# A decoder step on one core: the relative-position bias moves from matmuls to a VectorE addition, and attention's value products are issued for two pairs of heads at a time

## Chip, core and metric

The kernel runs on one core of a Trainium2 chip. The metric is the device time of one execution in microseconds (us). The engines are TensorE (PE; its weight loads are shown as PEld), VectorE (DVE), ScalarE (ACT), GpSimd (POOL) and SyncE (SP), which issues most transfers.

## The reference, cut to what matters

One hybrid layer: an input projection, sparse attention beside a gated linear recurrence (HGRN2), and an output projection. For the 1024 prompt rows, attention adds a relative-position bias to the logits of the keys that are kept:

```python
logits = jnp.einsum('btngd,btknd->btngk', qg, k_sel).astype(F32) * HEAD_DIM ** -0.5
bias = rel_table.astype(F32)[t5_bucket(q_pos[None, :, None] - idx)]   # 32 buckets, the last one from distance 128 on
logits = jnp.where(valid[:, :, None, None, :], logits + bias, -jnp.inf)
p = jax.nn.softmax(logits, axis=-1)
out = jnp.einsum('btngk,btknd->btngd', p.astype(v_sel.dtype), v_sel)
...
mix = jnp.concatenate([a_out * silu(a_gate), h_n * silu(h_gate)], axis=-1)
return x + jnp.einsum('bte,ed->btd', mix, w_out)
```

There are 8 query heads on 4 key/value heads. A bias that is the same for all far keys drops out of the softmax, so only the two 128-key blocks nearest to a query tile need one. Eight decode rows (the sample) go through the same layer against a paged cache.

## The kernel before

Everything up to about 560 us is projections, index search and recurrence. The change lives in what follows, `pe_tail`, `act_tail`, `dve_tail`, `gp_tail` and `sp_tail`, one instruction stream written out by hand for each engine and tied by semaphores.

The prompt's attention is a loop over **steps** m = 0 to 63. A step is one head (h = m mod 8) of one tile of 128 queries, t = 7 - m // 8, with the causal width of 128 (t + 1) keys, so the first eight steps are the widest (1024 keys) and the last eight the narrowest (128). In step m each engine does, in its own order:

- TensorE: the **scores** of head m + 1 (`scores`, L1139: keys as high and low part, `KA` L1154 and `KB` L1160, and between them two matmuls that add the bias, L1158, from `BH` and `BL`, its high and low part, against the antidiagonal matrix `ANR`); in odd steps from 3 on the **value products** of one pair of heads (`values`, L1178, matmuls on L1191); in some odd steps sample work (page keys L1251 in steps 3 to 15, page values L1294 in steps 25 to 35); the **transposes** of head m's probabilities (L1175); then the other sample work (`SIDE`), mixing (`mix`, L1195) and, from step 41, output products (`out`, L1210, matmuls on L1222). The last 23 groups of output products follow the loop.
- VectorE: the **maximum** of head m (L1093: adds the mask, writes the logits back to PSUM and reduces), for odd m from 19 on the copy of the transposed probabilities of head m - 1's turn (L1107), then its sample work: in the first dozen steps one round of a search of bits (`sample_keep` L928, `sample_try` L920), each of which waits for a small matmul on TensorE (L1235) that stands behind the transposes of the step.
- ScalarE: the **exponentials** of head m (L862), behind them the **copy** of the transposed probabilities of head m - 1 from PSUM (L874; in the steps where VectorE doesn't do it).

The scores of head m + 1 wait for the exponentials of head m - 1 (two halves of PSUM take turns). The transposes of head m wait for its exponentials and for the copy of head m - 1 (L1168 to L1170). A copy waits until its buffer, one of three (`PTS`), has been read by the value products. These read two heads:

```python
if m >= 3 and m % 2 == 1:
    values((m - 3) // 2)
```

The bias table leaves a matmul of L2042 as 8 rows of 383 distances, is stored to DRAM by SP (`bias_spill`, L1356, early in the program) and comes back spread over 128 partitions (L601). ScalarE rounds it (`act_bias`, L814) and VectorE takes the rest (L966) while the queries and keys are built (`dve_builds`), ahead of step 0.

## Time and profile before

| | us |
|---|---|
| median of 3 runs | 857.04 (856.95 to 860.72) |
| profiled execution, its own time | 857.15 |
| its span (first to last instruction) | 854.8 |
| TensorE busy in the span | 819.4 (96%) |
| VectorE busy | 570.8 (67%) |
| ScalarE busy | 410.6 (48%) |
| granted TensorE clock, mean | 1.0 of full speed |

A busy share is an average over stages with different limits. Matmuls are pipelined: the duration shown of one is its latency, and what it costs the engine is the distance from its start to the next one's.

### The profile page before, as it was taken

To read this page: it belongs to the slowest core of one execution; us is meant where nothing else is said; L and a number is where in the kernel's file an instruction comes from. 1 tells how busy PE (TensorE), PEld (TensorE's weight loads), DVE (VectorE), ACT (ScalarE), POOL (GpSimd) and SP (SyncE) were. 2 spreads that over 40 slices of the span, in tenths; PEclk is the share of its full clock that TensorE was granted. 3 is DMA by queue.
4 is the path that set the end of the run, shared out by engine and by line. 5 is a ranking of instruction groups with operands and counts; after the bars stand their busy time and mean duration, and the time that the engine had idled before them with its cause. 6 is when DMAs were issued, how large, how long until landed. Compare 5 with 4: busy or idle time off the path is not lost.

```text
span 854.8 us, 17930 instructions
## 1 busy us (share of the span) xinstructions
PE 819.4 (96%) x6497; PEld 741.2 (87%) x6497; DVE 570.8 (67%) x1153; ACT 410.6 (48%) x1200; POOL 384.0 (45%) x575
## 2 busy tenths in 40 slices
PE   3999989999999999999999999989999998999998
PEld 3989979699999989999999999956677667898998
DVE  4535777899988988859993536787856358555111
ACT  6646674224554496467455645554445345422100
POOL 2543635209824484549565425139731327501400
PEclk9999999999999999999999999999999999999999
DMA  8312102201101312041205145494653535341422
GB/s 268 80 38 60 62 27 68 76 21 50 51 2 50 98 53 75 26 130 39 82 26 150 37 117 150 130 257 124 158 161 122 162 99 167 107 142 45 142 76 75
DMA packets 69179, 81.31 MB, mean 95 GB/s; under 512 B 20234, under 2 KB 55738, under 8 KB 68842
## 3 DMA queue, kind: packets, MB, share of 16 engines
q1 hardware_dynamic: 64410, 66.58, 25.5%
q0 software_dynamic: 4688, 13.64, 5.8%
q8 instruction: 52, 0.85, 0.4%
q14 instruction: 29, 0.24, 0.1%
HBM read 62.85 MB, written 17.34 MB: 94 GB/s over the span
## 4 chain that ended last, share of the span: by engine, by line
PE 79%; issue 5%; DVE 4%; POOL 4%; ACT 3%; SPq 3%; DMA 2%; POOLq 0%; ACTq 0%; DVEq 0%
PE psum L2095 25%; PE psum L2092 15%; PE psum L1222 12%; PE psum L1991 4%; PE psum L2029 3%; PE psum L1175 3%; PE psum L1191 2%; PE psum L1294 2%; SPq L547 2%; PE psum L1975 2%; PE psum L2011 1%; PE psum L1158 1%; PE psum L1154 1%; PE psum L1160 1%; POOL page_keys L566 1%
## 5 line engine op out<-in xcount | busy, mean ns | idle before, releaser
L2095 PE MATMUL psum<-w_high,xT_high 128*128 128x256 f32 x720 | 204.1, 283 | 1.4 <-ACT psum L1672 1.4
L2095 PE MATMUL psum<-w_low,xT_high 128*128 128x256 f32 x720 | 201.9, 280 | 0.0
L2095 PE MATMUL psum<-w_high,xT_low 128*128 128x256 f32 x720 | 201.6, 280 | 0.0
L1878 DVE TENSOR_SCALAR_CACHE_REDUCE flag<-scores,candidate 128x384 f16<-128x384 f32 (+2 forms) x192 | 181.6, 946 | 6.8
L512 POOL TENSOR_TENSOR w_low<-w_raw,w_high 128x256 fp32r<-128x256 f32 (+1 forms) x168 | 123.0, 768 | 78.5 <-ACT w_high L1560 69.3
L2095 PEld LDWEIGHTS psum<-w_high,xT_high 128*128 128x128 f32 x720 | 127.4, 177 | 3.9 <-ACT psum L1672 1.6
L2095 PEld LDWEIGHTS psum<-w_low,xT_high 128*128 128x128 f32 x720 | 127.6, 177 | 2.3
L2095 PEld LDWEIGHTS psum<-w_high,xT_low 128*128 128x128 f32 x720 | 127.4, 177 | 2.4
L2092 PE MATMUL psum<-xT_high,w_high 128*128 128x384 f32 (+3 forms) x312 | 102.1, 327 | 1.6 <-DVE xT_low L1805 1.2
L2092 PE MATMUL psum<-xT_high,w_low 128*128 128x384 f32 (+3 forms) x312 | 99.7, 319 | 0.0
L2092 PE MATMUL psum<-xT_low,w_high 128*128 128x384 f32 (+3 forms) x312 | 99.6, 319 | 0.0
L862 ACT ACTIVATE prob<-psum,neg_max 128x1024 f32<-128x1024 f32 (+7 forms) x64 | 47.4, 740 | 98.9 <-DVE neg_max L1093 98.5
L1222 PE MATMUL psum<-w_high,xT_high 128*128 128x256 f32 (+1 forms) x288 | 81.9, 284 | 0.0
L1222 PE MATMUL psum<-w_low,xT_high 128*128 128x256 f32 (+1 forms) x288 | 80.7, 280 | 0.0
L1222 PE MATMUL psum<-w_high,xT_low 128*128 128x256 f32 (+1 forms) x288 | 80.6, 280 | 0.0
L1667 ACT ACTIVATE stage<-psum 128x256 f32<-128x256 f32 (+1 forms) x72 | 27.6, 385 | 86.4 <-PE psum L2095 76.8
L2092 PEld LDWEIGHTS psum<-xT_high,w_high 128*128 128x128 f32 (+1 forms) x312 | 57.6, 185 | 2.9 <-issue 1.2
L1462 POOL DMA_INDIRECT index_keys_T<-in_cache_ikt,index_page_rows x32 | 34.6, 1083 | 56.6 <-DMA index_keys_T<-in_cache_ikt,index_page_rows 55.7
L2092 PEld LDWEIGHTS psum<-xT_low,w_high 128*128 128x128 f32 (+1 forms) x312 | 57.6, 185 | 0.9
L2092 PEld LDWEIGHTS psum<-xT_high,w_low 128*128 128x128 f32 (+1 forms) x312 | 57.5, 184 | 0.5
L1093 DVE CUSTOM_DVE_ANT_0 psum<-psum,mask 128x1024 f32<-128x1024 f32 (+5 forms) x48 | 43.0, 898 | 19.1 <-PE psum L1160 18.4
L1003 DVE TENSOR_TENSOR y_rows<-psum,x_res 128x256 f32<-128x256 f32 (+1 forms) x36 | 15.1, 420 | 56.7 <-PE psum L1222 56.7
(313 smaller groups left out, 1853.5 us busy)
## 6 DMA issues: line engine op xcount, KB each, us to landing
w_raw<-in_w_main SPq DMA_DIRECT2D x40, 512.0 KB, 3.8
x_rows<-in_x_prompt SPq DMA_DIRECT2D x8, 512.0 KB, 5.6
page_keys<-in_cache_kt SPq DMA_DIRECT2D x32, 128.0 KB, 3.5
page_keys<-in_cache_kt POOLq DMA_DIRECT2D x32, 128.0 KB, 5.1
page_values<-in_cache_v SPq DMA_DIRECT2D x32, 128.0 KB, 3.7
page_values<-in_cache_v POOLq DMA_DIRECT2D x32, 128.0 KB, 3.4
x_res<-in_x_prompt SPq DMA_DIRECT2D x32, 128.0 KB
out<-y_rows SPq DMA_DIRECT2D x32, 128.0 KB
```

The lines of the kernel that those rows point to most:

```text
L512: last = gp.tensor_tensor(WL[:, u % 2, 4 * h + k, 0:w], WR[:, h, k, 0:w], f(WH[:, u % 2, 4 * h + k, 0:w]), ALU.subtract)
L862: act.activation(PB[:, m % 3, 0:w], ps(2 * (m % 2), w), ACT.Exp, scale=-1.0, bias=NB[:, h:h + 1], accum_out=RS[:, t % 2, h:h + 1]).then_in ...
L1093: dve.tensor_tensor_reduce(lg, lg, mask, -HD ** -0.5, 3e38, ALU.add, ALU.min, accum_out=NB[:, h:h + 1])\
L1175: last = pe.transpose(ps(4, P, o=b * P), PB[:, m % 3, b * P:(b + 1) * P], IDN[:, :])
L1222: last = pe.matmul(ps(OBANK[y], UW, rows(i)), a[:, k, row0(i):row0(i) + rows(i)], ww[:, sl, k, :], start=k == 0 and a is XH and ww is WH, ...
L1462: gp.indirect_dma_start(dst, None, cache_ikt.rearrange("a d k -> (a d) k"), bass.IndirectOffsetOnAxis(ap=PGX[:, col:col + 1], axis=0))\
L1667: last = act.activation(STG[0:r, g % 4, :], ps(bank, UW, r), ACT.Silu if kind in ("gh", "ga") else ACT.Copy)
L1878: dve.tensor_scalar(JK[:, 0:w], sc, threshold(k), None, op, ALU.add, accum_out=CNT[:, k:k + 1]).then_inc(s["dve_chain"], 1)
L1991: pe.matmul(ps(bank, 2 * SUB, w, o=2 * SUB * i), KT[:, o + c * w:o + (c + 1) * w], QT[:, :, c * P + i * SUB:c * P + (i + 1) * SUB], start= ...
L2029: last = pe.matmul(ps(4 + 2 * (m % 2) + c0 // 512, w), IQS[:, h, (t - 2) * P:(t - 1) * P], stack[:, c0:c0 + w], start=kk == 0, stop=kk == 1)
L2092: last = pe.matmul(ps(BANK[n], cw, m_), ww[:, sl, k, i * P:i * P + m_], x[:, k, t0:t0 + cw], start=first, stop=final)
L2095: last = pe.matmul(ps(BANK[n], w, rows(i)), x[:, k, row0(i):row0(i) + rows(i)], ww[:, sl, k, 0:w], start=first, stop=final)
```

## The change

TensorE no longer adds the bias. The table is stored to DRAM 128 times, once for each row of a tile, so that it can be read back with each row shifted by one (`BT`, in float32, in place of `BRAW`), and VectorE adds it to the scores in PSUM ahead of each maximum, waiting for that addition to end (`link`). ScalarE's rounding, VectorE's remainder, `ANR` and its load go away. In the space that is free, two more buffers of transposed probabilities stand (five), and the value products of two pairs of heads are issued together in the steps 5, 9, ... 61, the last two pairs behind the loop.

```diff
-        VT, BH, PT0, PT1, _e = over(H0, ("values_T", [NT, UW], F32), ("bias_high", [AH, NEAR], F32R),
-                                    ("pT_0", [NT, P], F32), ("pT_1", [NT, P], F32))
+        VT, PT3, PT4, PT0, PT1, _e = over(H0, ("values_T", [NT, UW], F32), ("pT_3", [NT, P], F32), ("pT_4", [NT, P], F32),
+                                          ("pT_0", [NT, P], F32), ("pT_1", [NT, P], F32))
-        PTS = [PT0, PT1, PT2]
+        PTS = [PT0, PT1, PT2, PT3, PT4]
-        d_ut = nc.dram_tensor("bias_spill", [AH, UL], F32)
+        d_ut = nc.dram_tensor("bias_spill", [AH, P, UL], F32)
...
-                sp.dma_start(BRAW[:, :, :], bass.AP(d_ut, 0, [[1, P], [UL, AH], [1, NEAR]])).then_inc(s["bias_in"], 16)
+                sp.dma_start(BT[:, :, :], bass.AP(d_ut, P - 1, [[UL - 1, P], [P * UL, AH], [1, NEAR]])).then_inc(s["bias_in"], 16)
...
-        def act_bias(act):
-            act.wait_ge(s["bias_in"], 16)
-            act.wait_ge(s["intra_products_ready"], NT * NG)
-            act.activation(BH[:, :, :], BRAW[:, :, :], ACT.Copy).then_inc(s["bias_high_ready"], 1)
...
-                    ge(act, s["attn_values_done"], (m1 - 1) // 2)
+                    ge(act, s["attn_values_done"], (m1 - 3) // 2)
...
-                if i == NT - 3:
-                    dve.wait_ge(s["bias_high_ready"], 1)
-                    dve.tensor_tensor(BL[:, :, :], BRAW[:, :, :], f(BH[:, :, :]), ALU.subtract).then_inc(s["bias_low_ready"], 1)
...
                     lg = ps(2 * (m % 2), P * (t + 1))
+                    k0, w = max(t - 1, 0) * P, min(t + 1, 2) * P
+                    if m == 0:
+                        dve.wait_ge(s["bias_in"], 16)
+                    link(dve.tensor_tensor(lg[:, k0:k0 + w], lg[:, k0:k0 + w], BT[:, h, NEAR - w:NEAR], ALU.add))
...
                     pe.matmul(ps(bank, n, o=c0), q, KA[:, h // 2, c0:c0 + n], start=True, stop=False)
-                    k0, k1 = max(c0, (t - 1) * P), min(c0 + n, (t + 1) * P)
-                    if k0 < k1:
-                        for half in (BH, BL):
-                            pe.matmul(ps(bank, k1 - k0, o=k0), ANR[:, :],
-                                      half[:, h, k0 - (t - 1) * P:k1 - (t - 1) * P], start=False, stop=False)
...
-                if m >= 3 and m % 2 == 1:
+                if m >= 5 and m % 4 == 1:
+                    values((m - 5) // 2)
                     values((m - 3) // 2)
...
+            values(NA // 2 - 2)
             values(NA // 2 - 1)
...
-            sp.dma_start(d_ut.ap(), UT[0:AH, :]).then_inc(s["bias_table_out"], 16)
+            sp.dma_start(d_ut.ap(), rep(UT[0:AH, :], P)).then_inc(s["bias_table_out"], 16)
```

TensorE, step 5 before: the scores of head 6 with their bias matmuls, then the first value products of heads 2 and 3 (pair 1; `pT_166` and `pT_185` are buffers of transposed probabilities).

```order
L1154 MATMUL psum<-kT_high,qT_stack 128x512
L1160 MATMUL psum<-kT_low,qT_stack 128x512
L1154 MATMUL psum<-kT_high,qT_stack 128x512
L1158 MATMUL psum<-bias_high,antidiagonal_r 128x256
L1158 MATMUL psum<-bias_low,antidiagonal_r 128x256
L1160 MATMUL psum<-kT_low,qT_stack 128x512
L1191 MATMUL psum<-pT_166,values_T 64x128
L1191 MATMUL psum<-pT_185,values_T 64x128
```

The same place of the changed kernel, whose own line numbers the rows show (L1146 and L1147 are the scores, L1178 the value products): the scores of head 6, then the first value products of heads 0 and 1 (`pT_183` and `pT_184` are buffers again).

```order
L1146 MATMUL psum<-kT_high,qT_stack 128x512
L1147 MATMUL psum<-kT_low,qT_stack 128x512
L1146 MATMUL psum<-kT_high,qT_stack 128x512
L1147 MATMUL psum<-kT_low,qT_stack 128x512
L1178 MATMUL psum<-pT_183,values_T 64x128
L1178 MATMUL psum<-pT_184,values_T 64x128
```

The bias matmuls are gone, and the pair that comes here is pair 0, which stood in step 3.

TensorE, step 5 before, where the value products end and the page keys begin.

```order
L1191 MATMUL psum<-pT_185,values_T 64x128
L1191 MATMUL psum<-pT_166,values_T 64x128
L1191 MATMUL psum<-pT_185,values_T 64x128
L1251 MATMUL psum<-page_keys_156,q_padded 32x512
L1251 MATMUL psum<-page_keys_157,q_padded 32x512
```

In the changed kernel, where the value products of heads 0 and 1 end, those of heads 2 and 3 follow.

```order
L1178 MATMUL psum<-pT_184,values_T 64x128
L1178 MATMUL psum<-pT_164,values_T 64x128
L1178 MATMUL psum<-pT_181,values_T 64x128
L1178 MATMUL psum<-pT_164,values_T 64x128
L1178 MATMUL psum<-pT_181,values_T 64x128
```

So step 5 holds 32 value products before and 64 now; the steps 3 and 7 hold none.

VectorE before, at the heads 0 to 2: the last product of the sample's new key, then the maximum of heads 0 and 1 (ISA, `neg_max`), and the first round of the search.

```order
L1011 TENSOR_TENSOR square<-q_rows_sample,k_rows_sample 8x4x64 x2
L1014 TENSOR_REDUCE new_key_scores<-square 8x8
L1093 ISA psum,neg_max<-psum,mask 128x1024
L1093 ISA neg_max 128x1
L1093 ISA psum,neg_max<-psum,mask 128x1024
L1093 ISA neg_max 128x1
L922 TENSOR_SCALAR candidate<-bits_so_far,candidate_bits,sign_flip 64x1
L924 TENSOR_SCALAR flag_sample,count<-scores_sample,candidate 64x1025
```

VectorE of the changed kernel at the same place (L1084 is the new addition, L1086 the maximum).

```order
L1000 TENSOR_TENSOR square<-q_rows_sample,k_rows_sample 8x4x64 x2
L1003 TENSOR_REDUCE new_key_scores<-square 8x8
L1084 TENSOR_TENSOR psum<-psum,bias_by_row 128x256
L1086 ISA psum,neg_max<-psum,mask 128x1024
L1086 ISA neg_max 128x1
L1084 TENSOR_TENSOR psum<-psum,bias_by_row 128x256
L1086 ISA psum,neg_max<-psum,mask 128x1024
L1086 ISA neg_max 128x1
L914 TENSOR_SCALAR candidate<-bits_so_far,candidate_bits,sign_flip 64x1
L916 TENSOR_SCALAR flag_sample,count<-scores_sample,candidate 64x1025
L918 TENSOR_SCALAR enough<-count 64x1
```

Ahead of each maximum now stands one addition over the two near blocks, 256 wide (128 in the last eight steps).

## Rows read from the trace of the kernel before

**Rows 1.** The page's first line: the span of the profiled execution.

```profile
span 854.8 us, 17930 instructions
```

**Rows 2.** Busy time by stretch: the loop (to 786 us) in three parts.

```profile
560.50:702.00 141.50, 133.62 (x1180) 96.71 (x1181) 89.98 (x189) 63.27 (x115) 66.16 (x121) 1.00 0.53 152
702.00:714.60 12.60, 9.64 (x89) 8.29 (x89) 10.64 (x19) 7.57 (x15) 6.71 (x7) 1.00 0.46 148
714.60:786.00 71.40, 68.89 (x611) 63.56 (x610) 40.85 (x108) 23.39 (x74) 24.31 (x24) 1.00 0.36 114
```

**Rows 3.** Timeline of TensorE in steps 3 to 5: start, us, [idle before].

```profile
577.45 0.33 PE L1175 MATMUL psum<-ident,prob 128*128 128x128 f32 x1
...
578.59 0.50 PE L1154 MATMUL psum<-kT_high,qT_stack 128*128 128x512 f32 x1
...
579.39 0.28 PE L1158 MATMUL psum<-bias_high,antidiagonal_r 128*128 128x256 f32 x1
579.51 0.28 PE L1158 MATMUL psum<-bias_low,antidiagonal_r 128*128 128x256 f32 x1
...
579.86 0.27 PE L1175 MATMUL psum<-ident,prob 128*128 128x128 f32 x1
...
582.46 0.33 PE L1191 MATMUL psum<-pT,values_T 128*64 128x128 f32 x2
...
584.36 0.62 PE L1251 MATMUL psum<-page_keys,q_padded 128*32 128x512 f32 x2
...
586.20 0.33 PE L1175 MATMUL psum<-ident,prob 128*128 128x128 f32 x1
```

**Rows 4.** Bias matmuls by source line: count, median ns, forms; one half of two.

```profile
L1158 PE MATMUL psum<-bias_high,antidiagonal_r x72: 220/279/288, 561.5 to 774.3; 128*128 128x256 f32 x48, 128*128 128x128 f32 x24
```

**Rows 5.** Timeline of TensorE, two bias matmuls 128 wide.

```profile
765.00 0.27 PE L1158 MATMUL psum<-bias_high,antidiagonal_r 128*128 128x128 f32 x1
765.11 0.27 PE L1158 MATMUL psum<-bias_low,antidiagonal_r 128*128 128x128 f32 x1
```

**Rows 6.** Timeline of VectorE: a search round begins, and the next maximum.

```profile
578.70 0.16 DVE L931 TENSOR_SCALAR bit_kept<-psum 64x1 int32<-64x1 f32 x1 [2.41 <-PE psum L1235]
...
580.97 1.23 DVE L1093 CUSTOM_DVE_ANT_0 psum<-psum,mask 128x1024 f32<-128x1024 f32 x1
```

**Rows 7.** Timeline of ScalarE: exponentials of one head, copy of another.

```profile
582.34 1.11 ACT L862 ACTIVATE prob<-psum,neg_max 128x1024 f32<-128x1024 f32 x1 [2.73 <-DVE neg_max L1093]
...
583.45 1.01 ACT L874 ACTIVATE pT<-psum 128x1024 f32<-128x1024 f32 x1
```

**Rows 8.** The page's groups: VectorE's nearest addition (count, busy, mean ns, idle before).

```profile
L1003 DVE TENSOR_TENSOR y_rows<-psum,x_res 128x256 f32<-128x256 f32 (+1 forms) x36 | 15.1, 420 | 56.7 <-PE psum L1222 56.7
```

**Rows 9.** Timeline ahead of step 0: VectorE's remainder, TensorE's first scores.

```profile
549.76 2.29 DVE L966 TENSOR_TENSOR bias_low<-bias_raw,bias_high 128x2048 fp32r<-128x2048 f32 x1
...
560.77 0.47 PE L1154 MATMUL psum<-kT_high,qT_stack 128*128 128x512 f32 x1 [0.96 <-DVE qT_stack L948]
```

**Rows 10.** Timeline of SP's queue around the bias table's store.

```profile
64.76 0.32 SPq L1356 DMA_DIRECT2D bias_spill<-bias_by_distance  x1
91.43 4.38 SPq L471 DMA_DIRECT2D w_raw<-in_w_main  x2
```

**Rows 11.** Timeline, places where TensorE waits (four) and GpSimd (one).

```profile
611.89 0.62 PE L1251 MATMUL psum<-page_keys,q_padded 128*32 128x512 f32 x2 [1.83 <-DMA page_keys<-in_cache_kt]
...
650.86 0.30 PE L1175 MATMUL psum<-ident,prob 128*128 128x128 f32 x1 [1.08 <-ACT pT L874]
...
702.00 0.63 PE L1207 MATMUL psum<-ident,agate_in 128*128 128x128 f32 x4 [0.36 <-ACT out_by_head L842]
...
707.89 1.29 POOL L743 TENSOR_TENSOR hgate_in<-hgate_in,hgrn_gain 128x512 f32<-128x512 f32 x1 [18.54 <-DMA agate_in<-agate_spill]
...
713.78 0.30 PE L1207 MATMUL psum<-ident,agate_in 128*128 128x128 f32 x1 [1.77 <-issue]
```

**Rows 12.** The chain that ended last: its last piece.

```profile
786.65 65.25 PE psum L1222 x552
```

More of the change, by code:

```diff
@@ L35 @@
 NEAR = 2 * P
-CONSTS_IN = 14 * 16
+CONSTS_IN = 13 * 16
 UL = 383
@@ L131 @@
 NUMBERS_AT = UNITS.index(("hg", 1))
-BIAS_AT = JOB0[LAST] + 12
 QUERIES_AT = JOB0[LAST] + 15
@@ L205, in hymba_step @@
         IDN = sb("ident", [P])
-        ANR = sb("antidiagonal_r", [P], F32R)
         QG = sb("q_gain", [HD])
@@ L329, in hymba_step @@
         assert _e <= cur[0]
-        TRF, ANT, _ = over(cur[0], ("causal_add_f", [P], F32), ("antidiagonal", [P], F32))
+        TRF, = over(cur[0], ("causal_add_f", [P], F32))[:1]
         VN, PN, DG, _e = over(cur[0] - 2048, ("v_new", [UW], F32), ("prob_new", [BR], F32), ("diag", [BR], F32))
@@ L350, in hymba_step @@
         RSM, _e = over(H0, ("relu_sample", [PAST + 1], F32))
-        BRAW, = over(R0_, ("bias_raw", [AH, NEAR], F32))[:1]
-        BL, = over(R0_, ("bias_low", [AH, NEAR], F32R))[:1]
-        VT, BH, PT0, PT1, _e = over(H0, ("values_T", [NT, UW], F32), ("bias_high", [AH, NEAR], F32R),
-                                    ("pT_0", [NT, P], F32), ("pT_1", [NT, P], F32))
+        BT, = over(R0_, ("bias_by_row", [AH, NEAR], F32))[:1]
+        VT, PT3, PT4, PT0, PT1, _e = over(H0, ("values_T", [NT, UW], F32), ("pT_3", [NT, P], F32), ("pT_4", [NT, P], F32),
+                                          ("pT_0", [NT, P], F32), ("pT_1", [NT, P], F32))
         assert _e <= cur[0], (_e, cur[0])
-        PTS = [PT0, PT1, PT2]
+        PTS = [PT0, PT1, PT2, PT3, PT4]
         PSA = ctx.enter_context(nc.psum_tensor("psum", [P, 8 * 512], F32))
@@ L873, in act_tail @@
                             act.wait_ge(s[f"rows_out{x}"], ALLS[x])
-                    act.activation(PTS[m1 % 3][:, :, :].rearrange("p b t -> p (b t)")[:, 0:w], ps(4, w), ACT.Copy)\
+                    act.activation(PTS[m1 % 5][:, :, :].rearrange("p b t -> p (b t)")[:, 0:w], ps(4, w), ACT.Copy)\
                         .then_inc(s["probs_T_act_ready"], 1)
@@ L1105, in dve_tail @@
                     dve.wait_ge(s["probs_transposed"], m1 + 1)
-                    ge(dve, s["attn_values_done"], (m1 - 1) // 2)
-                    dve.tensor_copy(PTS[m1 % 3][:, :, :].rearrange("p b t -> p (b t)")[:, 0:w], ps(4, w))\
+                    ge(dve, s["attn_values_done"], (m1 - 3) // 2)
+                    dve.tensor_copy(PTS[m1 % 5][:, :, :].rearrange("p b t -> p (b t)")[:, 0:w], ps(4, w))\
                         .then_inc(s["probs_T_dve_ready"], 1)
@@ L1144, in scores @@
                     pe.wait_ge(s["job_copied"], JOB0[NU])
-                    pe.wait_ge(s["bias_low_ready"], 1)
                     pe.wait_ge(s["masks_ready"], 6)
@@ L1191, in values @@
                         last = pe.matmul(ps(7, P, (g + 1) * HD, g * HD, kv * P), VT[:, b, kv * HD:(kv + 1) * HD],
-                                         PTS[(2 * p + g) % 3][:, b, :], start=b == 0, stop=b == t)
+                                         PTS[(2 * p + g) % 5][:, b, :], start=b == 0, stop=b == t)
                 last.then_inc(s["attn_values_done"], 1)
@@ L1310, in pe_tail @@
                     scores(m + 1)
-                if m >= 3 and m % 2 == 1:
+                if m >= 5 and m % 4 == 1:
+                    values((m - 5) // 2)
                     values((m - 3) // 2)
-                    for side in SIDE.get(m, ()):
-                        if side[0] in ("keys", "values"):
-                            sample(*side)
+                for side in SIDE.get(m, ()):
+                    if side[0] in ("keys", "values"):
+                        sample(*side)
                 transposes(m)
@@ L1346, in _ @@
                              (INM[:, :, :], c_masks[:, 0:256]),
-                             (HM[0:BR, :], c_masks[0:BR, 656:674]), (TRF[:, :], c_masks[:, 400:528]), (ANT[:, :], c_masks[:, 528:656])):
+                             (HM[0:BR, :], c_masks[0:BR, 656:674]), (TRF[:, :], c_masks[:, 400:528])):
                 sp.dma_start(dst, src).then_inc(s["const_in"], 16)
@@ L1477, in _ @@
             gp.wait_ge(s["const_in"], CONSTS_IN)
-            gp.tensor_scalar(ANR[:, :], ANT[:, :], 1.0, 0.0, ALU.mult, ALU.add)
             gp.tensor_scalar(E8B[0:8, :], E8[0:8, :], 1.0, 0.0, ALU.mult, ALU.add)
@@ L1752, in _ @@
                         chunk(*event)
-                    if n == BIAS_AT:
-                        act_bias(act)
                     if n in BUILD_AT:
```

## The prediction

> **What bounds the kernel now.** I read the chain that ended last first, then busy time by stretch, then TensorE's waits, and then the timelines of TensorE, VectorE and ScalarE side by side. The profiled span is 854.8 us [rows 1]. The reader is to see a loop that TensorE nearly fills but not quite: from 560.5 to 702.0 it is busy for 133.6 of 141.5 us, from 702.0 to 714.6 for 9.6 of 12.6, from there to 786.0 for 68.9 of 71.4 [rows 2]. So some 13 of 225 us are idle; all else that the change takes from TensorE is real time, if the other engines keep up. Behind the loop stands one block of output products of 65.25 us at the end of the chain [rows 12], which the change doesn't touch.
>
> One step of the widest tile shows how close the others are. The transposes of step 3 start at 577.45, the scores of head 5 at 578.59, the transposes of step 4 at 579.86; the value products of step 5 start at 582.46, its page keys at 584.36, its transposes at 586.20 [rows 3]. From step 3's transposes to step 5's it is 8.75 us, without a wait. In the same time VectorE does two search rounds of 2.27 us (578.70 to 580.97) and two maxima of 1.37 us (580.97 to ScalarE's start at 582.34) [rows 6, 7], 7.3 us in all. ScalarE needs 1.11 us for the exponentials and 1.01 for the copy behind them [rows 7].
>
> **What leaves TensorE.** 144 bias matmuls (two halves of 72): 96 are 256 wide, 48 are 128 wide [rows 4]. A wide one costs 0.12 us (579.39 to 579.51) [rows 3], a narrow one 0.11 (765.00 to 765.11) [rows 5]: 96 × 0.12 + 48 × 0.11 = **16.8 us**, 0.24 us in a usual step. That is the ceiling of the gain.
>
> **What comes to VectorE.** 64 additions in PSUM. The trace has no such operation; the nearest is an addition of a PSUM tile 256 wide to one in SBUF, 0.42 us [rows 8]. The range per addition: 0.35 (if its end overlaps what follows) to 0.5 (the wait for its end, of which I see up to 0.05 between tied VectorE instructions). I take 0.46, since it is the same read and the same width, tied to its successor: 64 × 0.46 = 29 us of VectorE time, less the remainder of 2.29 us [rows 9]. It stands in the path of every head: scores, addition, maximum, exponentials, transposes.
>
> **What moves.** The pairs 0, 2, 4, ... come two steps later, the others stay. Before, a pair's 1.9 us (582.46 to 584.36) lay between scores and transposes in every second step, and covered that path for both neighbours. Now it covers one step in four with 3.8 us, and the steps m = 3, 7, 11, ... have nothing unless sample work stands there. The five buffers never make a copy wait: it asks for the pair before the last but one.
>
> **What is nearly free.** The table's store grows from 12 KB to 1.57 MB at 64.76 us; SP's next transfer is at 91.43 [rows 10], so 26 us cover it. If the cover failed, the weights behind it would come as late as the store ends after that. The load keeps its size. Ahead of step 0, VectorE loses 2.29 us, but the last query tile needs TensorE's transposes first, and TensorE waited only 0.96 us there [rows 9]: I give 0.3. ScalarE's rounding and GpSimd's copy of the antidiagonal lie beside TensorE's projections: 0.
>
> **The sum, stretch by stretch** (a minus is earlier than before):
>
> Search steps, from step 5's transposes to step 9's. Before, two periods of 8.75 us: 17.4, the second a little shorter. After, from the end of step 5's transposes: round 5's result reaches VectorE at 0.15, a round 2.27, addition and maximum 1.8, exponentials 1.15 and copy 1.1 on ScalarE (the copy of head 6 stands behind the exponentials of head 7), transposes 0.95: step 7 ends at 7.4. Step 8 follows by the same queues: VectorE is still behind, its next round, addition and maximum end at 8.0, exponentials and copy at 10.1, transposes at 10.9. Step 9 has score 0.95, two pairs 3.8, page keys 1.84, transposes 0.85: 18.35. So these four steps become **0.95 slower**, though TensorE lost 0.95 us of work: the missing 1.9 is waits in steps 6 to 8. The first steps come out 1.2 late at step 5 and so +2.3 at step 9.
>
> Step 11 resets this. Before, TensorE waited 1.83 us for page keys until 611.89 [rows 11]; the pages depend on GpSimd's own work and not on the change. Now pair 4 (1.7 us) isn't in the way, so TensorE is there in time and leaves at the same 611.9, but owes pair 4: ±0.
>
> Steps 12 to 21. Scores save 10 × 0.24 = 2.4. The owed pair costs 1.7. Waits come at 12 (round, addition, maximum: 0.9), at 14 and 15 (0.4), at 19 and 20 (0.5 + 0.3) and at 21 (0.4): 2.5. Before, the transposes of step 21 start at 650.86 behind a wait of 1.08 [rows 11]. After: 2.5 + 1.7 - 2.4 = **+1.8**.
>
> Steps 22 to 35. Page values (1.83 us each) stand in every odd step from 25 on and cover the path. 14 steps save 14 × 0.24, and the tile with keys split at 512 saves 0.12 more in 8 of them: 4.3 us, of which two waits keep 0.9. Pair 17's neighbour (1.0) is deferred past step 35. So the last page values end 2.5 us early, **-2.5** where 702.00 stood [rows 11].
>
> Steps 36 to 39. TensorE's mixing at 713.78 waited 1.77 us; behind it stand GpSimd (18.54 us of waiting for `agate_in` until 707.89) and a VectorE operation [rows 11], a chain of transfers that starts when the last page values are copied out. It moves with that, so it stays at -2.5, and what the scores save here (1 us) is waited away.
>
> Steps 40 to 63. 24 × 0.23 = 5.3 us of scores leave. Against it: VectorE was without a pause behind the mixing and gets three additions there (+0.85); the steps 43 and 47 have no value products and only 0.7 to 1.6 us of TensorE work against a path of 2.0 + 0.46 (some 2 us); steps 45 and 49 wait 0.4 each; the one-block steps are covered by output products and keep 3 of their gain, but 1.5 of that ends in the step 51, 57 and 61 waits. Together about **+0.5**.
>
> Sum: -0.3 is absorbed at step 11; -2.5 + 0.5 = **-2 us**. Against the profiled execution's own 857.15, which is 0.1 above the median of 857.04, that gives 855. Its own range, from the two prices of the addition (0.35: some 2 us less in the uncovered steps; 0.5: 1 us more) and from the waits I followed (± 3 us): 850 to 859.
>
> **The rivals.**
>
> *The saving is mostly kept.* TensorE is busy for 94% of the first stretch and 96% of the last [rows 2], and VectorE has 51 of 141 us free there. If additions fit in its pauses and paths overlap better than I followed, 8 to 14 of the 16.8 us stay: 843 to 849, say 846. Against it: the cycle above. It decides if steps 6 to 8 show no wait of over 0.3 us.
>
> *VectorE and the path become the bound.* In the first stretch VectorE was busy 90.0 us; 36 additions of 0.46 make it 106.6 of 141.5. If every step without value products waits the addition's full 0.46 and, in addition, the 0.95 us that half a pair gave it, the 48 such steps lose 48 × 0.46 = 22, less 16.8: +5, 862; with two thirds of the steps waiting, the point from which it decides against the kernel, ±0 less 2. For it: the search steps. Against it: page values, page keys and output products cover half the steps. The Trainium skill (Perfetto Trace Analysis, Identifying the Most-Contended Engine) judges TensorE by the busy share of its weight loads rather than of its matmuls. The weight loads are busy 96.7 of 141.5 us [rows 2], 68%, against VectorE's 64% before and 75% after; by that page VectorE would then be the engine to relieve, and the time would come out as here, 862. No row before can show it.
>
> *It does nothing.* The waits at 611.89 and 713.78 [rows 11] are of transfers. If the page values' transfers, too, set the end at 702.00, step 36 starts where it did, and the loop behind it comes out even: 857.
>
> **How the numbers follow.** Forecast, -2: 0.50. Saving kept: 0.20. VectorE the bound: 0.20. Nothing: 0.10. A difference of over 0.5% (4.3 us) is about what a measurement of this kernel can tell from no change. Faster than that: the second case whole and 0.13 of the first, 0.33. Slower: 0.15 of the third case, and 0.01 of the first, 0.16. The rest is 0.51. The range 847 to 861 leaves out a good half of the second case and a third of the third, 0.2 in all.
>
> **What would show it.** Right: VectorE's additions at 0.40 to 0.48 us, 64 of them; TensorE's groups of L1154 and L1160 unchanged and 144 matmuls fewer; in the steps 7, 8 and 12 waits of TensorE for the copies of L874 of 1 us and more; page keys of step 11 at about 611.9 again; page values done about 2.5 us earlier; the block of 65.25 us unchanged. Wrong: TensorE's wait for L874 in total no larger than before (then the saving stays), or waits behind L1222 in the steps from 41 on of more than 3 us (then it is slower), or a late weight load near 91 us.

## The result: 3.7% slower, in two parts

The changed kernel takes 890.8 us (median of four executions, 885.25 to 895.11) against 857.3 for the kernel before. The ratio is 1.037, 95% interval [1.034, 1.040]. The forecast was 855 us, range 847 to 861: wrong in sign and in size. The profiled execution has a span of 893.2 us, against 854.8 [rows 1]. It is the slowest of the four (895.11 us), so the two parts below, read from it, add up to 38.4 us and not to the 33.5 of the medians.

**Part one lies ahead of the loop.** TensorE's first scores, which stood at 560.77 [rows 9], now start at 586.55, 25.8 us later, behind the same wait of 0.96 us for the same instruction of VectorE. Timeline of TensorE, changed kernel, the start of the loop (start, us, instruction, [idle before <- releaser]; a row with xN groups N instructions):

```profile
586.55 0.47 PE L1146 MATMUL psum<-kT_high,qT_stack 128*128 128x512 f32 x1 [0.96 <-DVE qT_stack L940]
...
587.10 0.39 PE L1146 MATMUL psum<-kT_high,qT_stack 128*128 128x512 f32 x1
587.33 0.40 PE L1147 MATMUL psum<-kT_low,qT_stack 128*128 128x512 f32 x1
...
591.04 1.43 PE L1162 MATMUL psum<-ident,prob 128*128 128x128 f32 x8 [2.40 <-ACT prob L854]
...
592.92 0.80 PE L1146 MATMUL psum<-kT_high,qT_stack 128*128 128x512 f32 x1
593.51 0.63 PE L1147 MATMUL psum<-kT_low,qT_stack 128*128 128x512 f32 x1
593.93 0.63 PE L1146 MATMUL psum<-kT_high,qT_stack 128*128 128x512 f32 x1
...
599.09 1.06 PE L1162 MATMUL psum<-ident,prob 128*128 128x128 f32 x8 [1.88 <-ACT pT L866]
...
603.68 1.91 PE L1238 MATMUL psum<-page_keys,q_padded 128*32 128x512 f32 x8 [2.29 <-DMA page_keys<-in_cache_kt]
```

Such a delay must be traced back to where it begins. GpSimd's timeline shows it: the gathers of index keys (each waits for the one before), between the weight work of two units.

```profile
64.89 1.00 POOL L1451 DMA_INDIRECT index_keys_T<-in_cache_ikt,index_page_rows  x1 [0.15 <-issue]
69.99 0.94 POOL L1451 DMA_INDIRECT index_keys_T<-in_cache_ikt,index_page_rows  x1 [4.10 <-DMA index_keys_T<-in_cache_ikt,index_page_rows]
86.41 1.18 POOL L1451 DMA_INDIRECT index_keys_T<-in_cache_ikt,index_page_rows  x1 [15.48 <-DMA index_keys_T<-in_cache_ikt,index_page_rows]
99.97 0.94 POOL L1451 DMA_INDIRECT index_keys_T<-in_cache_ikt,index_page_rows  x1 [12.39 <-DMA index_keys_T<-in_cache_ikt,index_page_rows]
102.68 1.84 POOL L1451 DMA_INDIRECT index_keys_T<-in_cache_ikt,index_page_rows  x1 [1.77 <-DMA index_keys_T<-in_cache_ikt,index_page_rows]
...
113.08 3.09 POOL L509 TENSOR_TENSOR w_low<-w_raw,w_high 128x256 fp32r<-128x256 f32 x3
```

The kernel before at the same place: the first and the last of the gathers behind 70 us, and the weight work behind them.

```profile
71.94 0.94 POOL L1462 DMA_INDIRECT index_keys_T<-in_cache_ikt,index_page_rows  x1 [1.88 <-DMA index_keys_T<-in_cache_ikt,index_page_rows]
...
85.77 1.12 POOL L1462 DMA_INDIRECT index_keys_T<-in_cache_ikt,index_page_rows  x1 [1.77 <-DMA index_keys_T<-in_cache_ikt,index_page_rows]
86.92 8.51 POOL L512 TENSOR_TENSOR w_low<-w_raw,w_high 128x256 fp32r<-128x256 f32 x8
```

And SP's queue of the changed kernel with the store, and the next weight load behind that work:

```profile
66.14 0.81 SPq L1345 DMA_DIRECT2D bias_spill<-bias_by_distance  x1
117.34 0.35 SPq L468 DMA_DIRECT2D w_raw<-in_w_main  x1
```

Two gathers wait 15.48 and 12.39 us where others need 1.8. They are the two that run beside the table's store. So GpSimd takes up the next unit's weights only at 113.08 and not at 86.92, and the weight load that stood at 91.43 [rows 10] comes at 117.34. In the next rows (busy time by window, before and changed; the last three columns are granted clock, DMA share, GB/s) the store shows as a DMA share of 0.46 that moves only 56 GB/s:

```profile
70.00:95.00 25.00, 25.00 (x149) 23.71 (x148) 16.73 (x24) 16.82 (x34) 14.38 (x15) 1.00 0.13 40
70.00:95.00 25.00, 25.00 (x152) 23.71 (x151) 15.97 (x28) 16.48 (x34) 2.10 (x2) 1.00 0.46 56
```

No row tells when the store lands. In windows of 5 us the share stays between 0.44 and 0.48 from 70 to 95 us, is 0.35 from 95 to 100 and 0.05 behind it; from the issue at 66.14 that makes some 33 us, an estimate.

**Part two lies in the loop.** From the first scores to the end of the span it is 306.7 us (893.2 - 586.55) against 294.0 before (854.8 - 560.77), 12.6 longer, although 144 products left TensorE. The three stretches of [rows 2], moved along:

```profile
586.30:737.60 151.30, 130.91 (x1085) 91.44 (x1086) 106.32 (x227) 63.35 (x116) 66.79 (x122) 0.94 0.51 145
737.60:749.50 11.90, 7.55 (x67) 6.23 (x66) 10.76 (x21) 6.88 (x14) 8.12 (x9) 0.82 0.55 171
749.50:823.60 74.10, 65.65 (x576) 61.00 (x575) 49.79 (x131) 24.14 (x74) 22.45 (x22) 0.96 0.33 104
```

The first stretch grew from 141.5 to 151.3 us, and TensorE idles 20.4 of it, not 7.9. The granted clock is 0.94, 0.82 and 0.96 where it was 1.00. In the timeline above the 512-wide products start 0.42 us apart at 593.51 (half level) and 0.23 apart at 587.10 (full clock). TensorE's waits from 584 us on, by line (total, times, longest):

```profile
PE psum L1162 <- ACT pT L866: 21.2, 17, 3.0
PE psum L1162 <- ACT prob L854: 3.4, 2, 2.4
PE psum L1162 <- DVE pT L1100: 3.2, 7, 0.7
```

Before, the wait for ScalarE's copies came to 4.9 us in 8 places. What did come as forecast: the additions, in the page's groups and at one place in VectorE's timeline, and the last block, unchanged [rows 12]:

```profile
L1084 DVE TENSOR_TENSOR psum<-psum,bias_by_row 128x256 f32<-128x256 f32 (+1 forms) x64 | 26.4, 413 | 27.1 <-PE psum L1147 26.3
```

```profile
599.09 0.43 DVE L1084 TENSOR_TENSOR psum<-psum,bias_by_row 128x256 f32<-128x256 f32 x1
599.55 1.23 DVE L1086 CUSTOM_DVE_ANT_0 psum<-psum,mask 128x1024 f32<-128x1024 f32 x1
```

```profile
825.15 65.25 PE psum L1209 x552
```

### The profile page after: what moved, and what is told of

Same layout as the page of the kernel before. It is cut to its first block, busy times and chain, and to the rows that moved or that the text cites. A ratio compares the mean times of both kernels' runs of the same rounds, so it can differ in the third digit from the quotient of the medians.

```text
span 893.2 us, 17700 instructions
## 1 busy us (share of the span) xinstructions
PE 819.5 (92%) x6353; PEld 737.0 (83%) x6353; DVE 608.1 (68%) x1216; ACT 409.5 (46%) x1199; POOL 389.1 (44%) x574
## 4 chain that ended last, share of the span: by engine, by line
PE 54%; issue 14%; DMA 12%; DVE 11%; POOL 5%; ACT 3%; SPq 1%; DVEq 0%; ACTq 0%; POOLq 0%
PE psum L2081 16%; PE psum L1209 11%; DMA index_keys_T<-in_cache_ikt,index_page_rows 9%; PE psum L2078 6%; PE psum L1178 4%; PE psum L1162 3%; POOL w_low L509 3%; DVE flag L1864 3%; PE psum L1977 3%; DMA page_keys<-in_cache_kt 2%; PE psum L1961 2%; DVE bit_kept L1878 1%; PE psum L1281 1%; PE psum L1146 1%; PE psum L1238 1%
## 5 line engine op out<-in xcount | busy, mean ns | idle before, releaser
L509 POOL TENSOR_TENSOR w_low<-w_raw,w_high 128x256 fp32r<-128x256 f32 (+1 forms) x168 | 127.4, 796 | 67.3 <-ACT w_high L1548 58.5
L2078 PE MATMUL psum<-xT_low,w_high 128*128 128x384 f32 (+3 forms) x312 | 99.6, 319 | 0.0
L1162 PE MATMUL psum<-ident,prob 128*128 128x128 f32 x288 | 47.0, 294 | 27.9 <-ACT pT L866 21.2
L1162 PEld LDWEIGHTS psum<-ident,prob 128*128 128x128 f32 x288 | 34.0, 149 | 44.6 <-ACT prob L854 24.5
```

The lines of the kernel that those rows point to most:

```text
L509: last = gp.tensor_tensor(WL[:, u % 2, 4 * h + k, 0:w], WR[:, h, k, 0:w], f(WH[:, u % 2, 4 * h + k, 0:w]), ALU.subtract)
L1162: last = pe.transpose(ps(4, P, o=b * P), PB[:, m % 3, b * P:(b + 1) * P], IDN[:, :])
L2078: last = pe.matmul(ps(BANK[n], cw, m_), ww[:, sl, k, i * P:i * P + m_], x[:, k, t0:t0 + cw], start=first, stop=final)
```

## Experiments

The theories: **A**, the 128-fold store holds up GpSimd's gathers and with them the projections. **B**, the doubled value products lay the path from scores to transposes bare. **C**, the additions on VectorE lengthen that path. **D**, waits bring the half clock with them. Medians are named against the kernel before as measured in the same series (858.6 to 859.7 us).

### 1 to 4: the store alone, and the store made cheap

The first is the kernel before with only this:

```
- sp.dma_start(d_ut.ap(), UT[0:AH, :])
+ sp.dma_start(d_ut.ap(), rep(UT[0:AH, :], P))      # [AH, P, UL]
```

> The kernel before with one edit: the bias table goes to DRAM 128 times, as in the changed kernel (1.57 MB instead of 12 KB, issued at the same place), and the load reads the first of the 128 copies. Nothing else is changed. Theory A (the store keeps DMA engines busy for some 33 us, GpSimd's chained gathers of index keys wait behind it, and the whole projection pipeline is late): about +26 us, 880 to 885, the first scores at about 586. Rival (the 26 us come from something else ahead of the loop, such as GpSimd's or ScalarE's moved work): within 3 us of before, 855 to 860, the first scores at 561.

Measured: 880.6 us, ratio 1.026 [1.023, 1.029], 21.5 us slower. The first scores start at 582.9, and from there to the end it is 875.0 - 582.9 = 292.1 us at full clock, against 294.0 before: the page keys of step 11, for which TensorE waited 1.83 us before, are there in time now. Two gathers wait as in the changed kernel:

```profile
85.39 1.26 POOL L1462 DMA_INDIRECT index_keys_T<-in_cache_ikt,index_page_rows  x1 [15.57 <-DMA index_keys_T<-in_cache_ikt,index_page_rows]
99.13 0.95 POOL L1462 DMA_INDIRECT index_keys_T<-in_cache_ikt,index_page_rows  x1 [12.47 <-DMA index_keys_T<-in_cache_ikt,index_page_rows]
```

That the store costs this much is shown by the time; that it goes through the gathers is read from the timeline. The second is the changed kernel with the copies made from DRAM to DRAM:

```
- sp.dma_start(d_ut.ap(), rep(UT[0:AH, :], P))
+ sp.dma_start(d_u1.ap(), UT[0:AH, :])
...
+ if u == 7:                                        # at about 273 us
+     sp.dma_start(bass.AP(d_ut, 0, [[UL, P], [P * UL, AH], [1, UL]]),
+                  bass.AP(d_u1, 0, [[0, P], [UL, AH], [1, UL]]))
```

> The changed kernel with a cheap way to the 128 copies: the small store of 12 KB where the kernel before had it, and a copy from DRAM to DRAM that makes 128 of it, issued at about 245 us, when the DMA engines are nearly idle. Theory A: the 26 us ahead of the loop go, and what is left is the loop's own loss of 12.6 us, so 868 to 872. If A holds and the loop's loss was itself a consequence of the late start (GpSimd's search and pages standing otherwise to TensorE): 853 to 860. If A is false: 885 to 892.

Measured: 870.6 us, 1.014 [1.010, 1.018]. So the store was worth 20.2 us of the changed kernel (890.8 - 870.6, two series), and the loop's loss stays without the late start. The third takes the doubling of the value products back besides:

```
- if m >= 5 and m % 4 == 1:
-     values((m - 5) // 2)
-     values((m - 3) // 2)
+ if m >= 3 and m % 2 == 1:
+     values((m - 3) // 2)
```

> The same cheap way to the 128 copies, the addition on VectorE and the five buffers kept, but the value products as in the kernel before: one pair of heads in every second step. Theory B (the doubling of value products in every fourth step lays bare the path from scores to transposes): 6 to 12 us faster than the run with the doubled products, about 857 to 862. Theory C (the addition on VectorE is what makes the loop slower, wherever the value products stand): within 3 us of the run with the doubled products. Theory D (both give waits, and the clock granted to TensorE falls after them): the clock comes back to 1.00 in this run alone, and the difference is over 8 us.

Measured: 860.6 us, 1.0017 [0.9999, 1.0035]: the doubling costs 10.0 us, theory B. The clock didn't come back whole (0.93 from 750 to 800 us), so D's condition isn't met.

> The changed kernel with its 128-fold store unchanged in form (from 8 partitions of SBUF), but issued at about 245 us instead of 66 us, where no gather of GpSimd is under way. Theory A (the harm is the meeting with the gathers): the first scores at 561 to 566, the time 868 to 875. If the store harms by holding up SP's own weight loads wherever it stands: the weight load behind it is late and the first scores stand at 570 or later. The store itself again takes 30 to 35 us.

Measured once: 891.0 us, the first scores at 586.3. The first case was wrong: moving the store past the gathers gained nothing. The second came: behind the store SP's own next transfers are late. SP's timeline shows it; below it the same place with the copy from DRAM:

```profile
272.35 0.80 SPq L1354 DMA_DIRECT2D bias_spill<-bias_by_distance  x1
314.38 0.40 SPq L1386 DMA_DIRECT2D ho_spill<-ho_rows  x1
```

```profile
272.94 0.62 SPq L1357 DMA_DIRECT2D bias_spill<-bias_rows  x1
292.07 0.39 SPq L1390 DMA_DIRECT2D ho_spill<-ho_rows  x1
```

`ho_rows` was complete at 274.0 and 274.6 us. Between the two issues SP's program has only the reading of 32 page numbers into registers left to do, and it takes 19 us with the cheap copy and 42 with the store (what couples the two I didn't try to find out). ScalarE's staging then waits 32.7 us for SP's spills and TensorE 24.6 for ScalarE. At both places the store harms, beside the gathers and ahead of SP's own work, so theory A names only one of its two ways.

### 5, 13, 14: why the store is slow

> As the run with single value products and the 128 copies made from DRAM to DRAM (860.6 us), but that copy is issued right behind the small store, at about 67 us, where the changed kernel has its 128-fold store. The bytes written and their pieces are the same as in the changed kernel; only the source is DRAM instead of 8 partitions of SBUF. Theory A, in its form that the source on 8 partitions makes the transfer slow: the copy lands within 10 us, GpSimd's gathers lose at most 5 us, and the time is 858 to 863. Rival (1.57 MB in pieces of 1532 bytes beside GpSimd's gathers is the trouble, whatever the source): the gathers again take 13 to 16 us each and the time is 878 or more.

Measured: 861.8 us, 1.0025 [0.9999, 1.005]. The copy landed 10.5 us after its issue at 68.8, and two gathers waited 3.85 and 5.42 us instead of 1.8. The bytes and their pieces are not the trouble. Two suspects were left: that the source is 8 partitions, and that the outermost dimension is 8. The Trainium skill (DMA: Bandwidth & Descriptors, Why a DMA increments its semaphore by 16 and not by 1) states that a transfer runs on the largest number of DMA engines, up to 16, that divides the outermost size of both source and target. With 8 outermost that is half of them, and a share of 0.46 looked like it.

> The run with single value products and the copy from DRAM to DRAM at about 270 us (860.6 us; that copy landed in 10.0 us at a DMA share of 0.96), with one edit: the copy walks its 8 heads outermost and the 128 copies inside, as the changed kernel's store does, instead of 128 outermost. Same bytes, same pieces, source still DRAM. Two theories of why the store from SBUF took some 33 us at a share of 0.46. Outermost dimension: a transfer is spread over as many engines as its outermost dimension allows, so with 8 it runs on half of the 16; then this copy shows a share near 0.5 and lands in 17 to 20 us, and the rest of the 33 us belongs to the source. Source (8 partitions of SBUF deliver slowly, whatever the order): this copy lands in 10 to 11 us at a share of 0.9 or more, as the other did. Time of the kernel: 860 to 863 by both, since no gather is near.

Measured: 861.5 us. Windows over this copy, and over the copy with 128 outermost (third experiment):

```profile
275.00:280.00 5.00, 5.00 (x44) 5.00 (x43) 4.28 (x12) 2.80 (x7) 1.83 (x3) 1.00 0.53 184
280.00:285.00 5.00, 5.00 (x44) 5.00 (x44) 4.32 (x10) 3.37 (x20) 3.80 (x6) 1.00 0.53 164
```

```profile
275.00:280.00 5.00, 5.00 (x44) 5.00 (x43) 4.28 (x12) 3.41 (x13) 2.44 (x4) 1.00 0.95 263
280.00:285.00 5.00, 5.00 (x44) 5.00 (x43) 4.28 (x12) 3.36 (x15) 3.19 (x5) 1.00 0.13 38
```

The Trainium skill's rule holds: share 0.53 against 0.95. But neither case had the time right: on half of the engines the copy still moves 164 to 184 GB/s and is over by 285, some 12 us behind its issue at 272.85, and doesn't take the 17 to 20 us of the first case. So the order of dimensions costs a few microseconds, and not 20.

> Single value products, and the changed kernel's store from SBUF at its old place (66 us), but issued as 8 stores of one head each, each from one partition to 128 rows. Same bytes, same pieces, same source. Outermost dimension: each store now has 128 outermost and runs on all 16 engines; if that was the whole trouble, all 8 are done within 10 to 17 us of the first at a share near 1, the gathers lose 5 to 10 us in all, and the time is 860 to 866. Source (a partition of SBUF is read slowly): the bytes still need 30 us or more, and one partition at a time is no better, rather worse: share high for 30 us, gathers at 12 to 16 us each, the time 878 to 890.

Measured: 899.0 us, 1.048 [1.044, 1.051], the slowest of all, and slower than the second case's 890. One window beside the stores:

```profile
75.00:80.00 5.00, 5.00 (x32) 4.75 (x31) 3.31 (x7) 3.51 (x10) 0.00 (x0) 1.00 0.86 28
```

All engines are occupied (0.86), and they move 28 GB/s, half of what they moved with 8 partitions at a time; the stores last from 66 to about 120 us, and three gathers wait 14.62, 12.40 and 19.26 us. So the source decides: eight partitions of SBUF deliver slowly, one at a time still more slowly, and more DMA engines on them are only occupied. SBUF as such isn't slow: in the second experiment's profile a store of 512 KB from all 128 partitions (`ho_spill`) landed in 3.9 us. Nor is the repetition alone, which the copies from DRAM have too. Whether reading one SBUF row 128 times adds to it no run separates from the small number of partitions.

### 6 to 8: the price of the additions

> Leaves the bias out altogether: no additions on VectorE and no bias products on TensorE; value products one pair in every second step, copy from DRAM to DRAM at 245 us or later, as in the run of 860.6 us. This prices the additions. Theory C (the additions take back what TensorE saves): 64 additions lie in the path often enough to cost 7 to 12 us, so 849 to 854. Rival (what TensorE saved was never worth anything, since other waits set the steps): within 3 us of 860.6.

Measured: 850.6 us, 0.990 [0.986, 0.993]. The additions cost 860.6 - 850.6 = 10.0 us where value products stand singly. All of TensorE's 16.8 us of bias products, gone without anything in their place, gave 8.4 to 8.6.

> Leaves the bias out altogether, with the value products of two pairs together in every fourth step, as changed (with the additions this took 870.6 us). Theory B (the doubled value products cost by themselves): 7 to 12 us slower than the same without bias and with single pairs. Rival (the doubling costs only because the addition lengthens the path that it lays bare): within 4 us of the single pairs, and some 15 us faster than with the additions.

Measured: 854.9 us, 0.994 [0.990, 0.9985]. So the doubling costs 4.3 us without additions and 10.0 with them; the additions cost 10.0 us singly and 15.7 (870.6 - 854.9) with the doubling. That is nearly the second case (within 4 us, some 15 us): together the two edits cost 5.7 us more than the sum of their prices alone. The executions of these kernels spread by some us; by my estimate from their spread the 4.3 is known to 3.5 us and the 5.7 to some 4.5, so both signs are likely and the sizes rough. From the first scores on, TensorE's waits for ScalarE's copies, in this order: no bias and single; no bias and doubled; additions and single; additions and doubled.

```profile
PE psum L1162 <- ACT pT L867: 8.9, 14, 1.6
```

```profile
PE psum L1162 <- ACT pT L867: 13.6, 15, 2.1
```

```profile
PE psum L1163 <- ACT pT L867: 15.2, 16, 2.1
```

```profile
PE psum L1163 <- ACT pT L867: 22.4, 18, 3.0
```

> As the run with single pairs and the copy from DRAM to DRAM at 67 us, but all copies of the transposed probabilities are made by ScalarE; before, VectorE made those of every odd step from step 19 on. VectorE loses some 22 copies of up to 1 us, and has the additions instead. If VectorE's queue is what the additions clog behind step 19: 3 to 6 us faster than single pairs alone, 853 to 857. If ScalarE's exponential and copy of one step, one behind the other, then set the step: 2 to 6 us slower.

Measured: 861.8 us, 1.0015 [0.9989, 1.004], as with VectorE's copies (861.8). Neither case came: moving 22 copies to ScalarE gives nothing and costs nothing. The waits for its copies are now 16.6 us in 22 places.

### 9, 10: half and half

```
 for half in (BH, BL):                       # h % 2 == 1: products with the identity
     pe.matmul(ps(bank, k1 - k0, o=k0), ANR[:, :], half[:, h // 2, ...])
...
+if h % 2 == 0:
+    link(dve.tensor_tensor(lg[:, b0:b0 + bw], lg[:, b0:b0 + bw], BRAW[:, h, NEAR - bw:NEAR], ALU.add))
```

> A mixture, on the ground of the kernel before (single value products, three buffers): the even heads get their bias by VectorE's addition, the odd heads by two products of TensorE with the identity (high and low part of the row-wise table, 8 KB together). The 128 copies are made from DRAM to DRAM at about 270 us. TensorE saves 8.4 us of its 16.8; VectorE gets 32 additions in the steps where it has no copy. If each step's cost is its own, half of both prices: 859 to 861, no change. If waits are at the steps where VectorE's addition meets its copy (odd steps from 19 on) and its search rounds, the even steps bear the addition more cheaply: 854 to 858, better than both kernels.

Measured: 857.8 us, 0.9977 [0.9963, 0.9991]: 1.9 us faster than the kernel before, and the only full version here that beats it and the changed one.

> The same mixture the other way round: additions on VectorE for the odd heads, whose steps carry the value products on TensorE and, from step 19 on, VectorE's copy of the transposed probabilities; products on TensorE for the even heads. If value products in the step cover the addition: 854 to 858, and better than the other mixture. If VectorE's queue decides (addition, maximum and copy in one step): 860 to 864, and worse than the other mixture by 2 to 5 us.

Measured: 860.5 us, 1.0018 [0.9998, 1.0038]. It is 2.7 us slower than the other mixture, as the second case said. Counted from head 0's exponentials the two profiles are 0.6 us apart at head 19, where VectorE's copies begin (77.2 and 77.8), and 4.6 at head 63 (209.1 and 213.7). So the addition belongs into steps in which VectorE has no copy.

### 11, 12: useless work in TensorE's waits

```
+for _ in range(2):
+    pe.matmul(ps(bank, k1 - k0, o=k0), q, KA[:, h // 2, k0:k1], start=True, stop=True)
 pe.matmul(ps(bank, n, o=c0), q, KA[:, h // 2, c0:c0 + n], start=True, stop=False)
```

> The run with doubled value products and the cheap copy (870.6 us), plus work that nobody needs: ahead of the scores of each head TensorE makes two products of the width of the old bias products (256 or 128 columns) into the same place, which the scores then overwrite. So TensorE has the work of the kernel before again (some 17 us), and VectorE's additions stay. In the profile of that run TensorE idled 36.4 us behind the first scores and its clock was at the half level for some 20 us. If the time is set by the path through VectorE and ScalarE, and the work only fills TensorE's waits: 868 to 875. If fewer pauses also bring the clock back (Theory D): faster than 870.6 by 2 to 8 us, 862 to 868, with the granted clock at 1.00 throughout. If TensorE's work is what counts: 880 to 888.

Measured: 871.1 us, 1.011 [1.005, 1.017]. Some 17 us of work more (144 products at the 0.12 us of the old ones, an estimate), and the time is the same (870.6). From 560 us to the end, without and with that work:

```profile
560.00:868.00 308.00, 271.61 (x2308) 222.28 (x2305) 183.58 (x408) 102.41 (x213) 111.76 (x171) 0.97 0.42 127
```

```profile
560.00:870.00 310.00, 282.39 (x2455) 235.09 (x2452) 185.20 (x408) 102.48 (x213) 111.77 (x171) 0.99 0.42 127
```

TensorE idles 27.6 us instead of 36.4, and the clock lost is less: summed over windows of 2 us, (1 - granted clock) times their length comes to 10.2 us without and 3.4 with the work. In this pair of profiles the added 17 us come out of the waits (8.8) and out of the half clock (6.8). The other executions agree on the clock: its mean over the whole kernel is 0.978 to 0.986 in the four without the work and 0.992 to 0.996 in the four with it. In both profiles each fall stands behind a wait of 1.5 us or more, but not every such wait is followed by one. In the run without the work the wait of 1.95 us at 576.67 is not (the window around it keeps 0.99), the one of 1.95 at 622.86 is:

```profile
576.67 1.06 PE L1163 MATMUL psum<-ident,prob 128*128 128x128 f32 x8 [1.95 <-ACT pT L867]
```

```profile
572.00:620.00 48.00, 40.28 (x306) 26.03 (x305) 40.31 (x95) 20.68 (x30) 37.26 (x62) 0.99 0.66 170
```

```profile
622.86 0.95 PE L1163 MATMUL psum<-ident,prob 128*128 128x128 f32 x7 [1.95 <-ACT pT L867]
```

```profile
620.00:624.00 4.00, 2.05 (x12) 1.60 (x13) 3.74 (x10) 1.91 (x3) 0.32 (x1) 0.96 0.00 0
624.00:628.00 4.00, 4.00 (x38) 3.44 (x38) 3.82 (x7) 2.72 (x4) 0.00 (x0) 0.61 0.00 0
```

Theory D in the form I wrote (faster, clock at 1.00 throughout) is false: the clock came back in part and no time was gained, because what the clock gave, the work took.

> The run with single value products and the cheap copy (860.6 us), with the same useless products ahead of each head's scores. In its profile TensorE idled 29.2 us behind the first scores and lost the equal of 5.1 us to the half clock. Path: 858 to 865. Theory D: 854 to 859, clock at 1.00 throughout. TensorE's work counts: 870 to 878. The difference to the run with doubled products also shows how much of the doubling's 10 us is clock: if it stays at 10, none of it.

Measured: 866.8 us, 1.0075 [1.0047, 1.0104], 6.2 us slower than without the work, between "path" and "TensorE's work". Here TensorE's work has a price of about a third. With the same work and the same lost clock (3.4 us in both profiles) the doubling costs 871.1 - 866.8 = 4.3 us, and not 10.0. The other 5.7 us of the 10.0 are time that TensorE's freed work was worth with single products (6.2) and is not with doubled ones (0.5), where it goes into waits and the half clock; how it splits between these two the runs don't settle.

## Why the prediction was wrong

The table counts from head 0's exponentials to those of a later head, in us, read from ScalarE's timeline.

| kernel | head 12 | head 24 | head 35 | head 48 | head 63 |
|---|---|---|---|---|---|
| before | 48.1 | 92.1 | 134.2 | 173.7 | 211.7 |
| additions, doubled, cheap copy | 53.5 | 99.0 | 141.5 | 183.7 | 221.9 |
| additions, single, cheap copy | 50.2 | 91.3 | 131.3 | 172.4 | 211.0 |
| no bias, single | 48.4 | 88.7 | 128.5 | 166.9 | 202.5 |
| changed | 54.2 | 99.6 | 143.7 | 185.0 | 223.1 |

**"What is nearly free": the store, costed at nothing. This step failed, and it is 20 to 22 us of the 32 to 33.** The sum has no term for it. I named as cover only SP's pause of 26 us [rows 10], and as price only a late weight load on SP. The 33 us of transfer were longer than the cover; above all, I asked which transfer follows in SP's queue, and not who else uses the DMA engines meanwhile. GpSimd's gathers do, one behind the other, with its weight work queued behind them. The sign I gave, a late weight load near 91 us, did show (117.34), as a consequence. The rows for it were in the trace: only 8 partitions were the source, and GpSimd's gathers stood beside.

**The terms per instruction were right.** Additions measured 0.413 us on average, 0.46 from start to start of the maximum, 64 of them. TensorE's 144 products are gone. The loads' and rounding's prices were small: the runs with the cheap copy start the loop between 560.7 and 564.6, a spread that I can't explain from these runs, against -0.3 forecast.

**The first search steps were sized about right.** I forecast +2.3 by step 9 (its parts, 1.2 and 0.95, make 2.15). With the cheap copy head 9's exponentials come 2.7 us late, counted from head 0. The waits for ScalarE's copies that I named as signs came, too: 1.0, 1.7 and 2.0 us in the steps 7, 8 and 12.

**"Step 11 resets this" failed.** With doubled products and the cheap copy, TensorE reaches step 11's page keys at 616.23, 52.2 us after its first scores (51.1 before), and doesn't wait there: it comes after the pages and not with them. The lag isn't taken up, and the owed pair comes on top: head 12 is 5.4 us late.

**Steps 12 to 35 failed in size.** I gave +1.8 at step 21 and then -2.5 at step 35. Measured: +6.8 at head 24 and +7.3 at head 35, so behind head 12 another 1.9 us were lost where I had a gain. I let the scores' 0.24 us per step come off in full wherever page values stood. But the saved products were themselves the cover: they stood in TensorE's queue while the path ran. Experiment 11 says it most sharply: putting all of their work back costs 0.5 us.

**Steps 36 to 63**: I gave +0.5; measured +2.9 more (10.2 at head 63). It is the same mistake in a smaller size: here, too, I took the scores' savings as gained.

**The clock had no term at all.** It was 1.00 throughout the profile before, and I took TensorE's durations as fixed. (Other executions of the kernel before, measured with the experiments, have a mean clock of 0.992 to 1.000, so it isn't free of it either.) With doubled products and the cheap copy 10.2 us are lost to it, in five stretches, each behind a wait of 1.5 to 3.1 us. I don't read this as an independent extra: in experiment 11 two thirds of it came back and the time stayed.

**Of the rivals**, "VectorE and the path become the bound" was the nearest (862, and 862 plus the store is 883). It gave the 48 steps without value products 0.46 us each in waits; the further 0.95 us that its text names isn't in its sum. Without the store the kernel is at 870.6, so the case, too, is 9 us low. Measured, TensorE's waits for ScalarE's copies rose from 4.9 to 22.4 us. The Trainium skill (Perfetto Trace Analysis, Identifying the Most-Contended Engine) judges TensorE's headroom by, among other things, the busy share of its weight loads. They were busy 91.4 of 151.3 us in the first stretch after the change, 60%, and VectorE 106.3, 70%: the trace agrees that VectorE has more of the stretch, as forecast (106.6). My chances were not consistent here: 0.15 of this case's 0.20 was to lie above 861.3, and yet the range up to 861 was said to leave out only a third of it.

Step by step from the kernel before to the changed one: the removed products -8.4 (-8.6 by the other series), additions 10.0, doubling 10.0, store 20.2, together 31.8. Measured are 31.8 (890.8 against 859.05 in the later series) to 33.5 us (857.3 in the first). This sum closes by construction, since each term is the difference of two neighbours on that way, and it proves nothing by itself. On another way the terms differ: doubling first is 4.3, and then the additions are 15.7.

## What to carry to other kernels

Ask of a transfer that grows not only what follows in its own queue, but who waits for the DMA engines while it lasts, and how many partitions of SBUF it reads: here 128 copies of 8 rows took some 33 us from SBUF and 10 from DRAM. Work taken from the busiest engine is a gain only where that engine had no wait right behind it; put back useless work of the same size, and the difference tells how much of it is on the path. In this kernel the value products, which two neighbouring steps shared as cover, were worth more spread over every second step than doubled in every fourth.

## What the hardware showed that I had not expected

- A store of 1.57 MB in pieces of 1532 bytes from 8 partitions of SBUF occupied 0.46 of the DMA engines for some 33 us, while all transfers together moved 47 to 62 GB/s. With the same bytes in 8 stores of one partition each the share was 0.86 and the rate in most windows 28 GB/s. From DRAM to DRAM they landed in 10.0 to 10.5 us.
- GpSimd's gathers, which waited 1.8 us each on little-used DMA engines (a share of 0.13), waited 12 to 16 us beside such a store, although it left half of the engines alone, and 12 to 19 us beside the eight stores.
- With the store in its queue, SP's next issue behind 32 register reads came after 42 us and not 19.
- TensorE's granted clock stayed at 1.00 through the loop in the profile of the kernel before. In the changed loop with the cheap copy it fell to the half level in five stretches, each behind a wait of 1.5 to 3.1 us; four other waits there of 1.6 to 2.0 us had no fall behind them. Two runs (the second and third experiment) whose programs are the same up to there, with the same wait of 2.4 us, differed in it: from 568 to 572 us the clock fell to 0.64 in the one and stayed at 1.00 in the other.
